# A bias load with a signal of its own, awaited ahead of the first scatter

## The chip, the cores and the metric

The kernel runs on one core of a Trainium2 chip. The metric is the device time of one execution in microseconds (us). The median of three runs of the kernel before is 1269.99 us (1265.9 to 1274.62).

## The reference, cut to what matters

One inference step of a hybrid layer: token mixers (gated delta rule and gated linear attention), a mixture of experts, and a final norm, all in float32, for 256 prompt tokens and 32 sample tokens. The mixture takes most of the time:

```
logits = x2d @ w_router + b_router                  # 288 tokens, 32 experts
top_v, top_i = lax.top_k(logits, 4); gates = softmax(top_v)
# for every expert e, over its tokens xe:
gu   = xe @ w_up[e] + b_up[e]                       # 1024 -> 2048
gate = minimum(gu[:, :1024], 7.0); up = clip(gu[:, 1024:], -7.0, 7.0)
act  = (up + 1.0) * gate * sigmoid(1.702 * gate)
yb   = act @ w_down[e] + b_down[e]                  # 1024 -> 1024
out[token] += yb * gates                            # then x += out, final rmsnorm by rms_final_w
```

## The kernel before

The five engines run programs of their own, ordered by semaphores written out by hand. After the token mixers and the router, the 32 experts are taken in 16 rounds of two experts, each expert with up to 64 token rows. The routine `two_experts` of each engine does one round.

**Weights.** A round needs 12 units of 2048 KB: four of w_up for each of the two experts, then two of w_down for each. They stream into a ring of eight slots. SP issues every load (`load_unit`, L354) in the order of use and, from unit 8 of the first round on (`refill`), each after a wait for the use that frees its slot. A unit of w_up is released by the last matmul that reads it. The units 0 to 7 of the first round are loaded while the mixers end; units 0 to 5 wait for places that the mixers free, unit 6 for slots of the state update, unit 7 (L375) for `out_done`, since its slot holds the new gated-delta state until POOL's store of it (L512, 2048 KB) has landed.

**SP's order around the change.** Four loads of the up bias into `b_gu` (L371), unit 6 (L373), the wait for `out_done`, unit 7, the wait for `yb_ok` (POOL's zeroing of `yr`, L514), the down bias into the first 32 rows of `yr` (L377, 128 KB), the final norm's gain into `wfin` on all partitions (L378, 512 KB), then the refills of units 8 to 11.

**TensorE.** After gathering the rows of the first two experts (`gather`, L999) it waits for `ld_bias` at 80, which counts the four loads of the up bias and the one of the down bias, 16 each (L1008), and for the last state update (L1009). Then the rounds: `up` of the first expert (bias matmuls at L958, weights at L971), in the first round only a turn of the gates, `scatter` (L950), `up` of the second expert, turns and gathers for the next round, `down` of both (L990). A scatter multiplies the matrix `S` by `yr`, the 128 output rows of the round before, and VectorE adds the result to `x2` (L1487). The first scatter takes no round's rows: `S` holds the gates and `yr` the down bias, zeros below, so that this product adds the down biases of all experts at once. Later scatters follow `rows_out`, which overwrites `yr`.

**wfin** is read at the end of the program only, behind a wait of VectorE for `ld_ffn` at 32; the first 16 of it are an early load of `wff`.

POOL issues its own stores of states: the gated-delta state (L512), then two of the prompt's and four of the sample's linear-attention state (L517, L521), 1152 KB in small rows.

Of the kernel before, what the change touches and what calls it, by code (L numbers as in the profile page):

```python
# [5 lines left out]
P = 128  # L6
# [21 lines left out]
E_N, TOPK, FF = 32, 4, 1024  # L28
# [8 lines left out]
def program(nc, a, o):  # L37
    ctx = ExitStack()
    with ctx:
# [3 lines left out]
        def sem(name):  # L43
            return ctx.enter_context(nc.semaphore(name))
# [21 lines left out]
        def share(s, rows, *shape):  # L66
# [50 lines left out]
        yr = xb[:, D:2 * D]  # L117
# [11 lines left out]
        wfin = hTf[:, 1280:1280 + D]  # L129
# [79 lines left out]
            rs8_ok qkn_ok p_qkT qkT_ok p_MA MA_ok p_y y_ok p_inv inv_ok  # L209
            p_tm p_ch ch_ok vd_ok p_smp g_abs g_exp g_lvl p_glvl p_low ag_ok  # L210
            ebl_ok zg_ok smk_ok smr_ok p_gkd kdg_ok p_gch gch_ok p_gs gsT_ok p_o0 p_gag og_ok slp_ok qs_e qs_ok sq_ok qksq_ok
            osq_ok o_ok p_oT oT_ok w_out w_out2 x_again p_x2 x2_ok xw_ok p_xnT
            xnT_ok p_lgT lgT_ok p_lg route_ok ss2_ok rs2_in xn_ok p_pos kdm_ok dec_ok p_up_s
            st_ok p_rows rows_ok hist_out out_done ld_ffn lg_ok tri_ok rnd_ok G_ok
            p_gat p_up p_yd p_sc p_S w_used gu_ok act_ok
# [17 lines left out]
        def place(n, odd):  # L233

            return (n + 4 * odd) % RING
# [21 lines left out]
        sems = {n: sem(n) for n in names}  # L257
# [38 lines left out]
        def _(sp):  # L296
# [50 lines left out]
            def load_unit(p, n, odd):  # L347

                if n < 8:
                    src = up[p * 2 + n // 4, n % 4 // 2, :, UNIT * (n % 2):UNIT * (n % 2 + 1)]  # L350
                else:
                    src = dn[p * 2 + (n - 8) // 2, n % 2]
                s = place(n, odd)
                sp.dma_start(slot[WSLOT[s]], src).then_inc(sems[f"ld_w{s}"], 16)  # L354
# [16 lines left out]
                sp.dma_start(b_gu[E_N * j:E_N * (j + 1)], a["b_up"][0, :, 512 * j:512 * (j + 1)]).then_inc(sems["ld_bias"], 16)  # L371
            sp.wait_ge(sems["p_up_s"], 4)
            load_unit(0, 6, 0)  # L373
            sp.wait_ge(sems["out_done"], 16 * 2)
            load_unit(0, 7, 0)  # L375
            sp.wait_ge(sems["yb_ok"], 1)
            sp.dma_start(yr[0:E_N], a["b_down"][0]).then_inc(sems["ld_bias"], 16)  # L377
            sp.dma_start(wfin, a["rms_final_w"].partition_broadcast(P)).then_inc(sems["ld_ffn"], 16)  # L378

            def refill(p, i, before, odd, n):  # L380

# [148 lines left out]
        def _(pe):  # L530
            c = Count(pe)

            def turn(out, src, n):

                return pe.transpose(out, src, ident[0:n, 0:n])  # L535
# [408 lines left out]
            def scatter(w, banks=(6, 7, 6, 7, 6, 7)):  # L944

                for at in range(6):
                    t, j = at // 2, at % 2
                    if banks[at] in banks[:at] or at < 2:
                        pe.wait_ge(sems["sc_ok"], w * 6 + max(at, 1))
                    pe.matmul(bank[banks[at]][0:TN[t], :], S[:, TO[t]:TO[t] + TN[t]], yr[:, 512 * j:512 * (j + 1)],  # L950
                              start=True, stop=True).then_inc(sems["p_sc"], 1)

            def up(i, q, k, odd):

                pe.wait_ge(sems["sel_ok"], i * 2 + (q + 1))
                for g in range(2):
                    rows_ = slice(64 * g, 64 * g + 64)
                    pe.matmul(bank[2 * q + g][:], sels[q][rows_].rearrange("p h c -> p (h c)"), b_gu[rows_], start=True, stop=False,  # L958
                              skip_group_check=True)
                for u in range(4):  # L960
                    n = 4 * q + u
                    if q == 0 and u % 2 == 0:
                        pe.wait_ge(sems["xe_ok"], i * 2 + (u // 2 + 1))
                    s = place(n, odd)
                    pe.wait_ge(sems[f"ld_w{s}"], landed(k, n, odd))
                    w = slot[WSLOT[s]].rearrange("p (k g h n) -> p k g h n", k=2, g=2, h=2)
                    for kk in range(2):
                        at = 2 * u + kk
                        for g in range(2):
                            for h in range(2):  # L970
                                last = pe.matmul(bank[2 * q + g][CAP * h:CAP * (h + 1), :], xeT[:, at, q * CAP:(q + 1) * CAP], w[:, kk, g, h, :],  # L971
                                                 start=False, stop=at == KT - 1, skip_group_check=True)
                    last.then_inc(sems["w_used" if u < 3 else "p_up"], 1)

            def act_t(q, w):

                pe.wait_ge(sems["act_ok"], w)
                for j in range(4):
                    last = turn(bank[5 - q][:, j * P:(j + 1) * P], by_cols(gu[:, 1])[:, :, j], P)
                last.then_inc(sems["p_at"], 1)  # L980

            def down(q, u, k, odd):

                n = 8 + 2 * q + u
                s = place(n, odd)
                pe.wait_ge(sems[f"ld_w{s}"], landed(k, n, odd))
                w = slot[WSLOT[s]].rearrange("p (k h n) -> p k h n", k=4, h=2)
                for kk in range(4):
                    for h in range(2):
                        last = pe.matmul(bank[5 - q][CAP * h:CAP * (h + 1), :], aTs[q][:, kk, CAP * u:CAP * (u + 1)], w[:, kk, h, :],  # L990
                                         start=u == 0 and kk == 0, stop=u == 1 and kk == 3, skip_group_check=True)
                last.then_inc(sems["w_used" if u < 1 else "p_yd"], 1)

            def gather(j, b):

                for n in range(4):
                    for t in range(NTT):
                        at = (4 * j + n) * P
                        last = pe.matmul(bank[b][:, n * P:(n + 1) * P], ot[:, t, at:at + P], G[:, t, :], start=t == 0, stop=t == NTT - 1)  # L999
                last.then_inc(sems["p_gat"], 1)  # L1000
# [4 lines left out]
            gather(0, 5)  # L1005
            pe.wait_ge(sems["lg_ok"], 5)
            gather(1, 4)
            pe.wait_ge(sems["ld_bias"], 80)  # L1008
            pe.wait_ge(sems["st_ok"], 6)  # L1009

            def two_experts(i, k, odd, first=False, last=False):

                up(i, 0, k, odd)
                if first:
                    pe.wait_ge(sems["gat_ok"], 1)
                    for t in range(NTT):
                        ins = turn(bank[5][0:E_N, TO[t]:TO[t] + TN[t]], gates[0:TN[t], E_N * t:E_N * (t + 1)], TN[t])
                    ins.then_inc(sems["p_gT"], 1)
                    pe.wait_ge(sems["rnd_ok"], 1)
                pe.wait_ge(sems["yb_ok"], i * 4 + 1)  # L1020
                pe.wait_ge(sems["S_ok"], i + 2)
                scatter(i)
                up(i, 1, k, odd)

                pe.wait_ge(sems["G_ok"], i * 2 + 2)
                for t in range(NTT):
                    ins = turn(bank[4][:, TO[t]:TO[t] + TN[t]], GG[0:TN[t], t, :], TN[t])
                ins.then_inc(sems["p_S"], 1)
                act_t(0, i * 2 + 1)
                if not last:  # L1030
                    pe.wait_ge(sems["G_ok"], i * 2 + 3)
                    pe.wait_ge(sems["sc_ok"], i * 6 + 7)
                    gather(0, 7)
                pe.wait_ge(sems["aT_ok"], i * 2 + 1)
                down(0, 0, k, odd)
                if last:
                    pe.wait_ge(sems["S_ok"], i + 3)
                    act_t(1, i * 2 + 2)
                    down(0, 1, k, odd)
                else:  # L1040
                    down(0, 1, k, odd)
                    pe.wait_ge(sems["S_ok"], i + 3)
                    act_t(1, i * 2 + 2)
                    gather(1, 6)
                pe.wait_ge(sems["aT_ok"], i * 2 + 2)
                down(1, 0, k, odd)
                down(1, 1, k, odd)

            two_experts(0, 0, 0, first=True)
            last = pe.value_load(rnd[0:1, 0:1], min_val=PAIRS // 2 - 1, max_val=5 * PAIRS // 2 - 1)  # L1050
            with pe.Fori(0, last) as m:
                two_experts(m * 2 + 1, m, 1)
                two_experts(m * 2 + 2, m + 1, 0)
# [789 lines left out]
```

## Time and profile before

| | before |
|---|---|
| median of the runs | 1269.99 us (3 runs, 1265.9 to 1274.62) |
| the profiled execution | 1268.15 us, its span 1266.4 us |
| TensorE (PE) busy | 1215.1 us, 96% |
| VectorE, ScalarE, GpSimd busy | 379.2, 215.3, 72.5 us |
| read from HBM, written | 428.39 MB, 4.88 MB |
| loads of w_up, w_down | 128 and 64 of 2048 KB |
| granted TensorE clock, mean | 0.979 |

Busy matmuls are pipelined and their ends are modelled, so a busy share of 96% doesn't say that TensorE is at its peak: matmuls behind a wait for weights also count as busy. The chain that ended last is followed back from the last instruction; at each step it names what released it. DMA share is the mean busy share of the core's 16 DMA engines; packets can overlap a little, so that a full stretch reads 1.0 or slightly above.

### The profile page before, as it was taken

Reading aid. Unit: us, or ns where it says so; the run is one execution under the profiler, and the core shown is the slowest. Engines: PE = TensorE matmul, PEld = TensorE weight load, DVE = VectorE, ACT = ScalarE, POOL = GpSimd, SP = SyncE. Lnnn points to the kernel's source line nnn. Section 1 sums busy time; section 2 is a strip of 40 time slices with the busy share of each in tenths; the row PEclk is TensorE's granted clock in tenths of the full one; section 3 lists DMA queues with packets and bytes.
Section 4 is the critical chain, followed back from the end, with each engine's and each line's share of the span. In section 5 each row is a group of like instructions: output and inputs, shape, how many; then the busy total and the mean of one; then the engine's idle time right before and its main releaser. Section 6 shows DMA issues by size and latency. Waiting matters only on the chain.

```text
span 1266.4 us, 15585 instructions
## 1 busy us (share of the span) xinstructions
PE 1215.1 (96%) x6209; PEld 591.7 (47%) x6209; DVE 379.2 (30%) x802; ACT 215.3 (17%) x522; POOL 72.5 (6%) x115
## 2 busy tenths in 40 slices
PE   6989999999599999999999999999999999999996
PEld 5777887757233434343433434343433424243432
DVE  3675874634030321212130321212130311212123
ACT  2144333412011101010111101010111101010102
POOL 5010103432000000000000000000000000000000
PEclk9999999897799999999999999999999999999999
DMA  9423010447699999999999999999999999999994
GB/s 270 138 84 120 7 68 1 146 171 308 230 399 427 427 427 427 429 428 429 428 427 430 429 427 427 430 429 428 428 430 429 427 429 430 429 427 429 429 429 195
DMA packets 49805, 433.75 MB, mean 343 GB/s; under 512 B 7422, under 2 KB 13898, under 8 KB 25196
## 3 DMA queue, kind: packets, MB, share of 16 engines
q1 hardware_dynamic: 48636, 429.59, 82.0%
q0 software_dynamic: 1136, 3.71, 1.0%
q8 instruction: 23, 0.38, 0.1%
q14 instruction: 10, 0.08, 0.0%
HBM read 428.39 MB, written 4.88 MB: 342 GB/s over the span
## 4 chain that ended last, share of the span: by engine, by line
PE 74%; DMA 19%; DVE 4%; ACT 1%; issue 1%; POOL 0%; DVEq 0%; SPq 0%; POOLq 0%; ACTq 0%
PE bank L971 30%; DMA ring<-in_w_up 13%; PE bank L990 11%; PE bank L950 7%; PE bank L999 4%; PE bank L594 4%; PE bank L535 3%; DMA ring<-in_w_down 3%; PE bank L686 3%; PE bank L864 2%; PE bank L958 2%; DMA out<-ring 1%; PE bank L743 1%; PE bank L765 1%; DMA xb<-in_b_down 1%
## 5 line engine op out<-in xcount | busy, mean ns | idle before, releaser
L971 PE MATMUL bank<-ring,xb 128*64 128x512 f32 x2048 | 450.6, 596 | 6.3 <-DMA ring<-in_w_up 6.3
L971 PEld LDWEIGHTS bank<-ring,xb 128*64 128x64 f32 x2048 | 144.6, 137 | 309.2 <-issue 299.6
L990 PE MATMUL bank<-ring,qkv 128*64 128x512 f32 x1024 | 227.2, 595 | 2.1 <-DMA ring<-in_w_down 1.4
L1487 DVE TENSOR_TENSOR qkv<-qkv,bank 128x512 f32<-128x512 f32 (+1 forms) x102 | 69.7, 683 | 295.0 <-PE bank L950 294.9
L990 PEld LDWEIGHTS bank<-ring,qkv 128*64 128x64 f32 x1024 | 70.7, 137 | 134.3 <-issue 127.7
L950 PE MATMUL bank<-xb,bT 128*128 128x512 f32 (+1 forms) x204 | 97.1, 611 | 1.6 <-DVE xb L1479 0.9
L999 PE MATMUL bank<-rowsel,ob 128*128 128x128 f32 x768 | 92.4, 278 | 0.0
L999 PEld LDWEIGHTS bank<-rowsel,ob 128*128 128x128 f32 x768 | 90.0, 195 | 0.3 <-issue 0.3
L1479 DVE COPY xb<-bank 64x512 f32<-64x512 f32 x16 | 11.1, 694 | 262.4 <-PE bank L990 262.4
L594 PE MATMUL bank<-hT,ring 128*128 128x288 f32 x320 | 81.0, 414 | 0.0
L1466 DVE TENSOR_SCALAR xb<-bank 128x512 f32<-128x512 f32 x32 | 21.8, 682 | 188.3 <-PE bank L535 188.3
L1769 ACT ACTIVATE qkv<-xb 128x512 f32<-128x512 f32 x32 | 20.2, 630 | 336.2 <-DVE xb L1466 334.1
L594 PEld LDWEIGHTS bank<-hT,ring 128*128 128x128 f32 x320 | 61.3, 193 | 17.6 <-issue 0.8
L1779 ACT COPY xb<-bank 64x512 f32<-64x512 f32 x48 | 27.8, 580 | 187.4 <-PE bank L990 187.0
L950 PEld LDWEIGHTS bank<-xb,bT 128*128 128x128 f32 (+1 forms) x204 | 26.8, 161 | 69.7 <-DVE qkv L1487 44.5
L524 POOL TENSOR_TENSOR rst<-rst,mhalf 128x1 f32<-128x1 f32 x3 | 2.6, 881 | 941.9 <-DVE rst L1562 941.8
L958 PE MATMUL bank<-hT 64*128 64x512 f32 x128 | 37.1, 656 | 13.6 <-DMA xb<-in_b_down 13.6
L1763 ACT ACTIVATE xb<-bank,wff 128x128 f32<-128x128 f32 x128 | 36.6, 369 | 55.1 <-PE bank L999 55.1
L1791 ACT COPY bT<-bank 128x288 f32<-128x288 f32 x16 | 6.4, 399 | 217.9 <-PE bank L535 217.9
L686 PE MATMUL bank<-hT,ring 128*128 128x288 f32 x128 | 40.0, 426 | 0.1
L864 PE MATMUL bank<-ring 128*128 128x512 f32 x64 | 30.8, 637 | 0.0
L535 PE MATMUL bank<-ident,xb 128*128 128x128 f32 x152 | 28.4, 305 | 1.6 <-DVE xb L1080 1.6
(342 smaller groups left out, 874.4 us busy)
## 6 DMA issues: line engine op xcount, KB each, us to landing
ring<-in_w_up SPq DMA_DIRECT2D x128, 2048.0 KB, 24.3
ring<-in_w_down SPq DMA_DIRECT2D x64, 2048.0 KB, 27.2
ring<-in_w_in SPq DMA_DIRECT2D x7, 2048.0 KB, 8.3
ring<-in_w_out SPq DMA_DIRECT2D x2, 2048.0 KB, 8.4
ring<-in_state_gdn SPq DMA_DIRECT2D x4, 512.0 KB, 10.0
out<-ring POOLq DMA_DIRECT2D x1, 2048.0 KB, 14.2
xb<-in_x_prompt SPq DMA_DIRECT2D x1, 1024.0 KB, 5.6
sls<-in_state_gla SPq DMA_DIRECT2D x4, 256.0 KB, 7.5
```

What stands on the lines that cost most here:

```text
L535: return pe.transpose(out, src, ident[0:n, 0:n])
L594: i = pe.matmul(bank[at % 4][:, 0:T], w[:, k, n * P:(n + 1) * P], hT[:, k, :], start=k == 0, stop=k == KT - 1)
L686: i = pe.matmul(bank[0][:, 0:T], w[:, k, n * P:(n + 1) * P], hT[:, k, :], start=k == 0, stop=k == KT - 1)
L864: i = pe.matmul(bank[b][:], z, w[:, k, :], start=k == 0, stop=k == KT - 1)
L950: pe.matmul(bank[banks[at]][0:TN[t], :], S[:, TO[t]:TO[t] + TN[t]], yr[:, 512 * j:512 * (j + 1)], start=True, stop=True).then_inc(sems["p_ ...
L958: pe.matmul(bank[2 * q + g][:], sels[q][rows_].rearrange("p h c -> p (h c)"), b_gu[rows_], start=True, stop=False, skip_group_check=True)
L971: last = pe.matmul(bank[2 * q + g][CAP * h:CAP * (h + 1), :], xeT[:, at, q * CAP:(q + 1) * CAP], w[:, kk, g, h, :], start=False, stop=at = ...
L990: last = pe.matmul(bank[5 - q][CAP * h:CAP * (h + 1), :], aTs[q][:, kk, CAP * u:CAP * (u + 1)], w[:, kk, h, :], start=u == 0 and kk == 0, ...
L999: last = pe.matmul(bank[b][:, n * P:(n + 1) * P], ot[:, t, at:at + P], G[:, t, :], start=t == 0, stop=t == NTT - 1)
L1487: v.tensor_tensor(d, d, bank[banks[at]][0:TN[t], :], ALU.add).then_inc(sems["sc_ok"], 1)
L1763: last = act.activation(xeT[:, k, :], bank[b][:, P * n:P * (n + 1)], ACT.Copy, scale=wff[:, k:k + 1])
L1779: act.copy(yr[CAP * q:CAP * (q + 1), 512 * h:512 * (h + 1)], bank[5 - q][CAP * h:CAP * (h + 1), :]).then_inc(sems["yb_ok"], 1)
```

## The change

The down bias gets a signal of its own, `ld_down`, in place of a name that nothing used. On SP, the load of wfin moves ahead of the wait for `out_done` and of unit 7, so that it follows unit 6; the down bias keeps its place behind unit 7 and the wait for `yb_ok`, and is now the last load ahead of the refills. TensorE waits ahead of the loop for the up bias alone (64), and, in the first round, for the down bias ahead of the first scatter, behind the first `up` and the turn of the gates.

```diff
-            osq_ok o_ok p_oT oT_ok w_out w_out2 x_again p_x2 x2_ok xw_ok p_xnT
+            osq_ok o_ok p_oT oT_ok w_out w_out2 x_again p_x2 x2_ok ld_down p_xnT
...
             sp.wait_ge(sems["p_up_s"], 4)
             load_unit(0, 6, 0)
+            sp.dma_start(wfin, a["rms_final_w"].partition_broadcast(P)).then_inc(sems["ld_ffn"], 16)
             sp.wait_ge(sems["out_done"], 16 * 2)
             load_unit(0, 7, 0)
             sp.wait_ge(sems["yb_ok"], 1)
-            sp.dma_start(yr[0:E_N], a["b_down"][0]).then_inc(sems["ld_bias"], 16)
-            sp.dma_start(wfin, a["rms_final_w"].partition_broadcast(P)).then_inc(sems["ld_ffn"], 16)
+            sp.dma_start(yr[0:E_N], a["b_down"][0]).then_inc(sems["ld_down"], 16)
...
             gather(1, 4)
-            pe.wait_ge(sems["ld_bias"], 80)
+            pe.wait_ge(sems["ld_bias"], 64)
             pe.wait_ge(sems["st_ok"], 6)
...
                     ins.then_inc(sems["p_gT"], 1)
                     pe.wait_ge(sems["rnd_ok"], 1)
+                    pe.wait_ge(sems["ld_down"], 16)
                 pe.wait_ge(sems["yb_ok"], i * 4 + 1)
                 pe.wait_ge(sems["S_ok"], i + 2)
                 scatter(i)
```

## Rows read from the trace of the kernel before

**Rows 1.** Page, part 2: what the DMA engines moved, in 40 equal slices of the span.
```profile
GB/s 270 138 84 120 7 68 1 146 171 308 230 399 427 427 427 427 429 428 429 428 427 430 429 427 427 430 429 428 428 430 429 427 429 430 429 427 429 429 429 195
```

**Rows 2.** Chain that ended last, late stretch. Columns: start us, length us, what.
```profile
1033.62 3.65 PE bank L971 x16
...
1058.15 34.15 DMA ring<-in_w_up
...
1092.34 3.65 PE bank L971 x16
...
1213.50 35.38 DMA ring<-in_w_down
...
1248.93 3.68 PE bank L990 x16
```

**Rows 3.** The same chain, ahead of the expert loop and in its first rounds.
```profile
307.15 14.24 DMA out<-ring
...
321.81 11.35 DMA xb<-in_b_down
...
333.20 2.08 PE bank L958 x4
335.28 16.02 PE bank L971 x64
...
352.43 5.76 PE bank L950 x12
...
359.25 13.88 PE bank L971 x64
...
394.44 1.06 PE bank L958 x4
...
451.27 1.06 PE bank L958 x4
```

**Rows 4.** Timeline of 296 to 375 us: start us, us, engine line op tiles [idle before].
```profile
302.79 18.97 SPq L354 DMA_DIRECT2D ring<-in_w_up  x2
...
312.51 7.10 PE L999 MATMUL bank<-rowsel,ob 128*128 128x128 f32 x48
...
319.65 1.14 ACT L1763 ACTIVATE xb<-bank,wff 128x128 f32<-128x128 f32 x4 [1.53 <-PE bank L999]
321.81 1.51 SPq L377 DMA_DIRECT2D xb<-in_b_down  x1
323.36 1.19 SPq L378 DMA_DIRECT2D hT<-in_rms_final_w  x1
...
341.04 10.63 SPq L354 DMA_DIRECT2D ring<-in_w_down  x4
...
363.11 10.97 SPq L354 DMA_DIRECT2D ring<-in_w_up  x4
```

**Rows 5.** Timeline of SP's queue alone, the first six weight units.
```profile
245.68 51.01 SPq L354 DMA_DIRECT2D ring<-in_w_up  x6
```

**Rows 6.** Windows: stretch, length, engines' busy us (count), PEclk, DMA share, GB/s.
```profile
300.00:320.00 20.00, 19.62 (x151) 18.18 (x150) 12.62 (x52) 7.55 (x13) 7.47 (x11) 0.66 1.01 384
320.00:326.00 6.00, 0.00 (x0) 0.00 (x0) 0.00 (x0) 0.80 (x4) 0.00 (x0) 0.71 0.98 265
326.00:332.00 6.00, 0.00 (x0) 0.00 (x0) 0.00 (x0) 0.00 (x0) 0.00 (x0) 0.50 0.94 331
332.00:342.00 10.00, 8.80 (x26) 2.59 (x28) 0.00 (x0) 0.00 (x0) 0.00 (x0) 0.62 0.07 27
342.00:344.00 2.00, 2.00 (x12) 0.70 (x10) 0.00 (x0) 0.00 (x0) 0.00 (x0) 1.00 0.95 238
...
362.00:366.00 4.00, 4.00 (x20) 1.29 (x18) 0.68 (x3) 0.00 (x0) 0.00 (x0) 1.00 0.57 164
...
400.00:1200.00 800.00, 795.11 (x3786) 312.90 (x3784) 165.34 (x364) 96.04 (x224) 0.00 (x0) 1.00 1.01 428
```

**Rows 7.** Tile in_w_up: time from issue to landing over its 128 loads.
```profile
DMA to landing us min/median/max: 7.2/24.3/34.4
```

## The prediction

> **What bounds the kernel now.** I read the page's slices first. From the thirteenth slice on (380 us) the DMA engines move 427 to 430 GB/s in every slice up to the last [rows 1]: one stream of expert weights. The reader is to see that this rate does not vary, whatever the engines do meanwhile.
>
> The chain that ended last says who waits for whom at the end. TensorE starts the same part of a round at 1033.62 and at 1092.34, so a round of two experts takes 58.72 us there, and the round holds one link in which a weight load is the cause, 34.15 us long; the last weight unit releases TensorE at 1248.93 [rows 2]. The end is set by the weight stream. Earlier it is not: between 394.44 and 451.27 a round takes 56.83 us and no load appears in the chain [rows 3]. TensorE alone needs 56.83 us a round, the stream 12 units of 2.097 MB (2048 KB), at the 428 GB/s of the slices [rows 1] 4.90 us each, 58.8 us. TensorE lives on the eight slots of the ring until its lead is used up, and from then on the stream decides. So whatever is gained ahead of the loop counts at the end only as far as the weight stream ends sooner.
>
> The same chain shows the place of the change. The state store occupies 307.15 to 321.39, then the down bias 321.81 to 333.16, then the first matmul of the loop at 333.20 [rows 3]. The timeline shows that TensorE had ended its gather at 319.61 (312.51 plus 7.10) and stood still for 13.59 us [rows 4]. SP's queue had issued units 0 to 5 by 296.69 [rows 5], and unit 6 at 302.79; unit 7 went out at 321.42, behind the store, b_down right behind it at 321.81, and wfin at 323.36 [rows 4]. The next weight unit (unit 8) goes out only at 341.04, when the first up unit has been used [rows 4].
>
> The windows show what that does to the stream. From 300 to 332 the DMA engines are full (shares 1.01, 0.98, 0.94), although at 265 to 384 GB/s, since the state stores are among the work; then 10 us with a share of 0.07, and again 4 us from 362 with 0.57; from 400 to 1200 the share is 1.01 [rows 6]. The first hole is the late first up. The second comes from the four units issued at 341.04 to 351.67 being drained before the next four are released at 363.11 [rows 4].
>
> **The change, part by part.**
>
> The wait ahead of the loop falls from 80 to 64: b_up alone. Its four loads stand ahead of unit 6 in SP's queue, issued before 302.79 [rows 4]; the 16.8 us to 319.61 exceed the shortest landing of a whole weight unit, 7.2 us, and the median under full load, 24.3, belongs to a queue of many units that is not there [rows 7]. Units 0 to 3 are older still. The other condition inside the first up is ScalarE's second half of the gathered rows, done at 320.79 [rows 4] and wanted half-way through, about 327. So TensorE starts at 319.65 and not at 333.20.
>
> It also runs faster. After the standstill the granted clock is 0.50 and only 0.62 over 332 to 342 [rows 6], the lower level of 1.2 GHz in part; the bias matmuls took 2.08 us against 1.06 later and the 64 up instructions 16.02 against 13.88 [rows 3]. Together 13.55 + 1.02 + 2.14 = 16.7 us for TensorE. The Trainium skill (TensorE: Matmul & The Clock Gate, section "Part 1: The HAM clock gate") states that a TensorE that stands still falls to half clock and gets it back by sustained work; the trace agrees (0.50 over 326 to 332), and by it 3.2 of those 16.7 us go with the wait. If the clock stayed low instead, the same work would cost those 3.2 us as before, and the sum below would still hold, as its slack shows.
>
> What the 16.7 us are worth is read from the stream. The first up ends each unit 3.47 us (13.88/4) after the one before: releases at 324.2, 327.6, 331.1, 334.6. The DMA engines are full until 332.7 (332 plus 0.07 x 10 us), so units 8 to 11 queue behind that work and run to 332.7 + 4 x 4.90 = 352.3. The fifth release needs the gate turn and copy (352.43 - 351.30 = 1.13 us), the scatter (5.76), the bias (1.06) and a unit (3.47) [rows 3]: 346.0, and its packets flow 1.1 us later (issue at 341.04; the share of 0.95 over 342 to 344 begins about 342.1): 347.1, with 5.2 us to spare. After that TensorE frees twelve slots in 56.83 us and the stream fills twelve in 58.8, so the lead grows. Both holes close.
>
> The size of the holes, from two sides. By engine time: 10 x (1.01 - 0.07) + 2 x (1.01 - 0.95) + 4 x (1.01 - 0.57) = 9.4 + 0.1 + 1.8 = 11.3 us [rows 6]. By bytes: 0.27 + 0.48 + 0.66 = 1.41 MB moved in those 16 us, at 428 GB/s 3.3 us' worth, so 12.7 us. I take 11.3, since engine time is what the stores and loads ahead of the hole use up and keep using.
>
> The wfin load moves ahead of the wait for the store, unit 7 and b_down. SP issues it (1.19 us) while it would wait until 321.4 anyway: nothing. Its 512 KB, at the 384 GB/s of 300 to 320 [rows 6], are 1.4 us of DMA that now stand before 332.7 rather than at its end; the full stretch ends at the same time. The store, unit 7 and b_down land up to 1.4 us later. If the engines were not full there, it would fill a gap, a gain of at most 1.4.
>
> b_down and the new wait. It goes out behind unit 7 as before and lands at 333.2 to 334.6 (11.35 us after issue, plus wfin's 1.4). TensorE comes to the new wait at about 335.1, ScalarE's copy follows the signal given ahead of it and ends at 335.7, so the wait costs 0. Queued behind it on TensorE are the scatter, the second up and all later releases; VectorE's gains wait for those. If b_down is late, the first 5.2 us of that are covered as above, and each further one opens a hole again. From below: no wait, and none of it gained. From above: b_down as slow as the median unit in the deep queue, 24.3 us [rows 7], plus 1.4: 347.5, 11.8 us late, 6.6 beyond the slack, gain 4.7. I take 0, as the row of b_down itself is nearest.
>
> The Trainium skill (DMA: Bandwidth & Descriptors, section "Queues, rings and completion order") states that each engine takes a queue's descriptors in ring order and turns between queues packet by packet; by it units 8 to 11, behind b_down in SP's queue, cannot hold it back, and only POOL's stores share with it. The trace agrees so far that 128 KB behind a 2 MB unit took 11.35 us.
>
> Sum: -11.3 us. The profiled execution took 1268.15 us, its span 1266.4 (1.75 around it), so 1256.9; the median of the runs shown, 1269.99, lies 1.8 above the profiled one, so 1258.7 on its scale.
>
> **Rivals.**
>
> A, the stream gains more. For it: TensorE is 16.7 us ahead, and 320 to 332 runs at 265 and 331 GB/s, mean 298 [rows 6]; if weight units queued behind unit 7 lifted that to 428, 12 x 130/428 = 3.6 us more: 15.0, hence 1255.0; with the full 16.7, 1253.3. Against: the engines' share there is already 0.94 to 0.98.
>
> B, b_down late. The wait moves from ahead of the loop to ahead of the scatter; two fifths of the stream's gain stay: 4.7, hence 1265.3. For it: it still stands behind unit 7, with wfin ahead too. Against: its own landing and 5.2 us of slack.
>
> C, the other side: b_down as late as the slowest unit, 34.4 us [rows 7]. 321.81 + 34.4 + 1.4 = 357.6, 21.9 behind 335.7, 16.7 beyond the slack; the hole is then larger than the 11.3 it replaced, slower by 5.4: 1275.4. It decides from a landing past 352.2. Nothing in the rows has such a queue ahead of 332.
>
> D, the change doesn't do it: another signal holds the first up. The latest seen is ScalarE at 320.79; even a hold until 327.6, 8 us, would open a hole of only 2.8 us beyond the slack. For no change it must last to 333. 1270.
>
> **How the numbers follow.** Forecast 0.72, its own range 1257.3 (12.7) to 1260.0 (10.0); A 0.13; B 0.10; C 0.02; D 0.03. The likeliest gives 1258.7. The three runs of before spread over 1265.9 to 1274.62, so I add some 2 us below A's mean and stop at B: 1253 to 1265.5. About 1% is what a measurement of this kernel can tell from no change; that is 12.7 us. All of A and a third of the forecast pass it: 0.13 + 0.24 = 0.37, as faster; C and a rest 0.03 as slower; the other 0.60 within.
>
> **What would show it.** Right: the first bias matmul at about 319.7; unit 8 issued at about 324, near unit 7; DMA share about 1.0 through 332 to 366; the first up at 13.9 us; b_down's landing at 333 to 335 and at most 1 us of TensorE idle ahead of the first scatter; the last unit's release at 1237.6 (1248.93 - 11.3). Links of weight loads enter the chain in an earlier round than before. Wrong: a link of b_down in the chain, a hole in the windows between 332 and 366, or a stream below 428 GB/s after it.

## The result and the profile after

The changed kernel takes 1258.9 us (median of nine runs, 1253.9 to 1268.67) against 1269.99 before: 0.9923 of before, with a 95% interval of 0.9895 to 0.9950, that is 9.8 us less (6.3 to 13.3). This ratio, which the text goes by, is not that of the two medians, which lie 11.1 us apart. Beside later experiments it ran again at 0.9921 (0.9890 to 0.9953) and at 0.9910 (0.9875 to 0.9946). The forecast was 1258.7, the gain forecast 11.3 us. All three ratios lie within 1% of before, their intervals on both sides of it. Of all runs below one is left out, a slow one of 2884.84 us among the eleven with the stores moved.

The profiled execution after took 1258.68 us, its span 1257.0, so 9.47 below the one of before. The slices of the page after, to be held against [rows 1]:

```profile
GB/s 271 137 82 119 14 68 1 95 224 251 367 427 427 426 429 427 428 430 428 429 428 428 430 427 430 429 428 428 430 428 429 428 429 430 427 429 429 427 427 185
```

A slice is 31.4 us here. The level is the same, but it is reached one slice earlier: the eleventh slice (314 to 346 us) moves 367 GB/s where it moved 230, the twelfth 427 where it moved 399.

The windows of after, in the same stretches as [rows 6] (length, engines' busy us, granted clock, DMA share, GB/s):

```profile
300.00:320.00 20.00, 19.22 (x129) 17.76 (x129) 11.57 (x41) 6.09 (x8) 5.66 (x8) 0.55 0.98 389
320.00:326.00 6.00, 6.00 (x41) 5.46 (x40) 1.81 (x13) 1.75 (x7) 2.25 (x4) 0.79 1.02 311
326.00:332.00 6.00, 6.00 (x30) 1.95 (x30) 0.00 (x0) 0.53 (x3) 0.00 (x0) 1.00 0.96 316
332.00:342.00 10.00, 9.32 (x45) 3.12 (x42) 0.00 (x0) 0.84 (x2) 0.00 (x0) 1.00 1.02 390
342.00:344.00 2.00, 2.00 (x6) 0.61 (x4) 1.26 (x2) 0.83 (x1) 0.00 (x0) 1.00 0.98 418
344.00:362.00 18.00, 18.00 (x76) 5.46 (x74) 6.45 (x16) 0.63 (x1) 0.00 (x0) 1.00 1.01 428
362.00:366.00 4.00, 4.00 (x35) 3.60 (x33) 2.46 (x4) 1.62 (x3) 0.00 (x0) 1.00 0.99 420
...
400.00:1200.00 800.00, 792.91 (x3775) 311.93 (x3774) 164.84 (x364) 96.05 (x224) 0.00 (x0) 1.00 1.01 428
```

The reader is to see the second column from the right. The stretch of 332 to 342 had a share of 0.07 and has 1.02; that of 362 to 366 had 0.57 and has 0.99; the stream of 400 to 1200 is as it was, 428 GB/s. Both holes are gone and no other appears.

SP's queue in the timeline of after (start us, length us, line, tiles):

```profile
303.79 1.73 SPq L371 DMA_DIRECT2D hT<-in_b_up  x4
307.50 0.35 SPq L354 DMA_DIRECT2D ring<-in_w_up  x1
307.89 0.43 SPq L374 DMA_DIRECT2D hT<-in_rms_final_w  x1
324.74 0.33 SPq L354 DMA_DIRECT2D ring<-in_w_up  x1
325.12 1.48 SPq L378 DMA_DIRECT2D xb<-in_b_down  x1
330.04 10.63 SPq L354 DMA_DIRECT2D ring<-in_w_down  x4
352.11 21.46 SPq L354 DMA_DIRECT2D ring<-in_w_up  x6
```

POOL's store of the state in the same timeline:

```profile
309.85 1.75 POOL L512 DMA_DIRECT2D out<-ring  x1 [6.37 <-DVE ring L1379]
```

Unit 8 follows unit 7 by 5.3 us (324.74 to 330.04), where it followed by 19.6 (321.42 to 341.04, [rows 4]). All that SP issues is some 3 to 5 us later than before, unit 6 at 307.50 against 302.79 and POOL's store of the state at 309.85 against 307.15: in this execution the mixers ended later, and the granted clock over 300 to 320 was 0.55 against 0.66. No instruction that the change touches lies ahead of that. From the start of the store to the last unit's release it is 1239.49 - 309.85 = 929.64 us against 1248.93 - 307.15 = 941.78 [rows 2, 3]: 12.1 less, of which the later store takes 2.7 back. Before and after, one execution each; the same stretch of the other executions stands at the end of the experiments.

The chain of after around the place, and at the end (start us, length us, what):

```profile
317.29 8.06 PE bank L999 x48
325.35 1.06 PE bank L958 x4
326.41 13.88 PE bank L971 x64
...
340.79 0.40 ACT bT L1786
341.19 0.25 issue
341.43 5.76 PE bank L950 x12
...
1239.49 3.68 PE bank L990 x16
```

TensorE goes from the gather straight into the bias matmuls, which take 1.06 us, not 2.08, and the first up takes 13.88, not 16.02 [rows 3]. ScalarE's copy, not the bias, releases the first scatter; no link of b_down is left in this chain. The tile's view says that the bias landed 12.5 us after its issue, at 337.6, and TensorE wanted it at 341.4:

```profile
DMA to landing us min/median/max: 12.5/12.5/12.5
```

### The profile page after: what moved, and what is told of

Its sections match the earlier page's. It is cut to its first block, busy times and chain, and to the rows that moved or that the text cites. A ratio compares the mean times of both kernels' runs of the same rounds, so it can differ in the third digit from the quotient of the medians.

```text
span 1257.0 us, 15585 instructions
## 1 busy us (share of the span) xinstructions
PE 1218.6 (97%) x6209; PEld 596.6 (47%) x6209; DVE 379.2 (30%) x802; ACT 215.2 (17%) x522; POOL 72.5 (6%) x115
## 4 chain that ended last, share of the span: by engine, by line
PE 74%; DMA 20%; DVE 4%; ACT 1%; issue 1%; POOL 0%; DVEq 0%; SPq 0%; POOLq 0%; ACTq 0%
PE bank L971 29%; DMA ring<-in_w_up 16%; PE bank L990 10%; PE bank L950 7%; PE bank L999 4%; PE bank L594 4%; PE bank L535 3%; DMA ring<-in_w_down 3%; PE bank L686 3%; PE bank L864 2%; PE bank L958 2%; PE bank L765 1%; PE bank L848 1%; PE bank L743 1%; PE bank L752 1%; PE bank L750 1%
## 5 line engine op out<-in xcount | busy, mean ns | idle before, releaser
L1480 DVE COPY xb<-bank 64x512 f32<-64x512 f32 x16 | 11.1, 694 | 262.4 <-PE bank L990 262.4
```

## The experiments

Two theories. **Stream**: the end is set by the weight stream; the change is worth the holes that it closes in it, and TensorE's earlier start is worth nothing beyond that. **Start**: the time follows how early and how fast TensorE enters the loop. A smaller rival gives wfin's move a part of the gain. Ratios are to runs of the kernel before on the same chip, medians 1271.67, 1271.48 and 1275.64 in the three groups. Each diff is against the changed kernel, that of wfin alone against the kernel before.

### The wait split alone

```diff
             load_unit(0, 6, 0)
-            sp.dma_start(wfin, ...)
             sp.wait_ge(sems["out_done"], 16 * 2)
...
             sp.dma_start(yr[0:E_N], a["b_down"][0]).then_inc(sems["ld_down"], 16)
+            sp.dma_start(wfin, ...)
```

> The wait is split as in the change, but wfin keeps its place behind b_down. Stream theory (the end is set by the weight stream, and the change closed the holes in it): wfin's 512 KB are the same DMA work on either side of unit 7, so the whole gain stays, about 11 us off the kernel before (1259 of 1270). Rival, wfin's move is part of the gain: 1.4 us or more of it is missing. In the profile: DMA share about 1.0 from 332 to 366, no wait for b_down ahead of the first scatter.

Measured: 1260.45 us, 0.9920 (0.9890 to 0.9949). The share of 332 to 342 is 1.02:

```profile
332.00:342.00 10.00, 9.32 (x45) 3.12 (x42) 0.00 (x0) 0.94 (x2) 0.00 (x0) 1.00 1.02 393
```

The gain comes from the split wait. A part of 1.4 us for wfin's place is smaller than the interval and is not excluded by these times; the next run bears on it, and so does the table at the end of the experiments.

### The wfin move alone

```diff
             load_unit(0, 6, 0)
+            sp.dma_start(wfin, ...)
...
             sp.dma_start(yr[0:E_N], a["b_down"][0]).then_inc(sems["ld_bias"], 16)
-            sp.dma_start(wfin, ...)
```

> Only wfin moves; TensorE still waits for the down bias ahead of the loop. Stream theory: the hole of about 11 us stays and b_down lands up to 1.4 us later, so 1270 to 1271.4, no change that can be told. Rival, wfin's move carries the gain: 1260 to 1265.

Measured: 1273.35 us, 1.0022 (0.9999 to 1.0044), so no gain. Its windows still have the hole, and TensorE stands still before it at the low clock:

```profile
326.00:334.00 8.00, 0.00 (x0) 0.00 (x0) 0.00 (x0) 0.00 (x0) 0.00 (x0) 0.50 0.83 311
334.00:344.00 10.00, 8.36 (x24) 2.44 (x26) 0.00 (x0) 0.00 (x0) 0.00 (x0) 0.60 0.01 3
```

### TensorE early, the stream late

```diff
+            sp.wait_ge(sems["w_used"], 4)
             for n in range(RING, 12):
                 refill(0, 0, 0, 0, n)
```

> The change, with SP holding back units 8 to 11 until the first unit of the second up is used. TensorE starts the loop as early as with the change, but the stream gets a hole of about 14.4 us (332.7 to 347.1 on the clock of the trace before), against 11.3 before. Stream theory: the gain is gone, 1270 to 1273. Rival, TensorE's earlier start (16.7 us) is what pays: 1253 to 1259, as with the change.

Measured: 1275.07 us, 1.0031 (1.0003 to 1.0058). This run separates the theories. The chain shows the loop entered as early and as fast as with the change (lines stand one further down), and the windows of the same execution show the stream's hole:

```profile
320.76 1.06 PE bank L959 x4
321.81 13.88 PE bank L972 x64
...
336.83 5.76 PE bank L951 x12
```

```profile
326.00:332.00 6.00, 6.00 (x30) 2.01 (x28) 0.00 (x0) 0.00 (x0) 0.00 (x0) 1.00 0.91 348
332.00:348.00 16.00, 15.32 (x59) 4.69 (x57) 7.71 (x17) 2.30 (x3) 0.00 (x0) 1.00 0.03 11
348.00:352.00 4.00, 4.00 (x22) 1.37 (x20) 0.00 (x0) 0.00 (x0) 0.00 (x0) 1.00 0.94 315
```

TensorE is busy over the whole stretch (15.32 of 16 us, granted clock 1.00), the DMA engines are not (0.03), and the time is that of the kernel before and a little more, 4.0 us (0.4 to 7.4). That fits the larger hole: by bytes, as in the prediction, the 0.18 MB of 332 to 348 leave 15.6 us empty, against 12.7 before. The start pays nothing that these runs can tell.

### The down bias behind one unit, and behind four

```diff
-            sp.dma_start(yr[0:E_N], a["b_down"][0]).then_inc(sems["ld_down"], 16)
-            for n in range(RING, 12):
+            refill(0, 0, 0, 0, RING)
+            sp.dma_start(yr[0:E_N], a["b_down"][0]).then_inc(sems["ld_down"], 16)
+            for n in range(RING + 1, 12):
                 refill(0, 0, 0, 0, n)
```

> The change, with the down bias loaded behind unit 8. It lands 4 to 6 us after TensorE reaches the new wait. Stream theory: that lies within or just beyond the slack of 5.2 us, so the time of the change stays to within 1 us (1259 to 1260), while TensorE shows the wait ahead of the first scatter. Rival, every us of TensorE's start counts: 4 to 6 us above the change, 1263 to 1265.

Measured: 1259.18 us, 0.9906 (0.9870 to 0.9942), beside the change at 0.9921. The wait is there and costs nothing that can be told. The chain of its profiled execution (1267.83 us, the longest of its six):

```profile
332.48 3.61 PE bank L972 x16
...
336.52 14.24 DMA xb<-in_b_down
350.76 0.09 issue
350.85 7.20 PE bank L951 x12
358.05 1.06 PE bank L959 x4
```

The first up would have let the scatter begin at about 347.5 (332.48 + 13.88, and the 1.13 of the turn and copy), so TensorE stood for 3.3 us. The scatter then took 7.20 us, not 5.76 (the granted clock was 0.86 over 350 to 362), so that the second up began 4.8 us late, within the slack of 5.2. The windows show a trace of a hole at the place where the fifth release is due, 0.4 us (2 x 0.21):

```profile
350.00:362.00 12.00, 11.15 (x30) 3.62 (x32) 7.16 (x15) 0.63 (x1) 0.00 (x0) 0.86 1.00 425
362.00:364.00 2.00, 2.00 (x12) 0.72 (x10) 0.55 (x3) 0.00 (x0) 0.00 (x0) 1.00 0.80 320
```

With all four units ahead of the bias:

```diff
-            sp.dma_start(yr[0:E_N], a["b_down"][0]).then_inc(sems["ld_down"], 16)
             for n in range(RING, 12):
                 refill(0, 0, 0, 0, n)
+            sp.dma_start(yr[0:E_N], a["b_down"][0]).then_inc(sems["ld_down"], 16)
```

> The change, with the down bias loaded behind units 8 to 11. It lands about 19 us after TensorE reaches the new wait, 13.7 us beyond the slack of 5.2, and TensorE restarts at half clock, up to 3 us more. Stream theory: a hole of 14 to 17 us comes back, 1272 to 1276. Rival, TensorE's start pays in full: 19 to 22 us above the change, 1278 to 1281.

Measured: 1272.64 us, 1.0009 (0.9981 to 1.0037). The bias is awaited from about 341.4 (the first up's end at 340.27 and the 1.13) until 358.67, 17.3 us; the stream then runs empty:

```profile
326.36 13.91 PE bank L971 x64
...
340.65 18.02 DMA xb<-in_b_down
```

```profile
340.00:356.00 16.00, 0.70 (x5) 0.20 (x3) 0.00 (x0) 1.67 (x2) 0.00 (x0) 0.67 1.00 426
356.00:372.00 16.00, 13.24 (x39) 4.20 (x40) 7.71 (x17) 0.63 (x1) 0.00 (x0) 0.80 0.04 14
```

While TensorE stands, the stream is full (1.00); 16 us later, when TensorE works, it is empty (0.04), a hole of 15.5 us. The gain is gone, as in the forecast's rival C, though the time is about 1 us above before and not the 2 to 6 expected; the interval reaches to 4.7 us. By the prediction's own sum a stand of 17.3 us costs 17.3 - 5.2 - 11.3 = 0.8 us against before. So a bias that came 3.3 us late was free, and one that came 17.3 us late took the gain away; between the two nothing was run.

### The stores out of the way

This asks whether taking DMA work out of the full stretch ahead of the stream moves the end. POOL's stores of slp and sls become SP's, behind the last weight unit:

```diff
-            g.wait_ge(sems["gch_ok"], 2)          # POOL, ahead of the loop
-            ... 2 stores of slp; wait for st_ok; 4 stores of sls
...
             for n in range(12):
                 refill(PAIRS - 1, last * 2 + 1, last * 2, 1, n)
+            sp.wait_ge(sems["gch_ok"], 2)
+            ... the same 6 stores
```

> The changed kernel once more, beside the next three on one chip. About 0.992 of before, near 1259 of 1270.

Measured: 1260.29 us, 0.9921 (0.9890 to 0.9953). In this execution the mixers ended some 6 us earlier than in the one shown above (the first bias matmul at 319.18 against 325.35), and the down bias was the last to come, by little: the scatter began at 335.40, where the copy alone would have let it begin at about 335.25 (319.18 + 1.06 + 13.88 + 1.13).

```profile
322.93 12.39 DMA xb<-in_b_down
335.31 0.09 issue
335.40 5.76 PE bank L950 x12
```

> The change, with POOL's stores of the linear-attention states (slp and sls, 1152 KB) issued by SP behind the last weight unit instead of ahead of the loop, where those stores moved 281 GB/s alone (321 to 324 us of the trace before): 4.2 us of DMA work leave the full stretch ahead of the stream, and TensorE's work is the same. Stream theory: 4 us below the change, near 1255, as the last 17 us of the kernel have room for the stores. Rival, TensorE's start sets the time: no difference to the change, 1259.

Measured: 1260.05 us, 0.9911 (0.9878 to 0.9945). That is 1.3 us below the change beside it by the ratios and 0.2 by the medians; the intervals are too wide to tell either from 0 or from the 4 expected. The profiled executions tell more. The one here can be laid over that of after: its chain has the bias matmuls' work begin 0.15 us later (the first up at 326.56 against 326.41). Its last unit is released at 1238.16, 1.33 earlier, in this one pair. Its windows show where the rest went:

```profile
320.00:332.00 12.00, 12.00 (x68) 7.53 (x69) 1.93 (x14) 2.29 (x8) 0.00 (x0) 0.89 0.83 305
...
332.00:350.00 18.00, 17.29 (x67) 5.35 (x65) 5.91 (x9) 2.30 (x3) 0.00 (x0) 1.00 0.98 418
350.00:356.00 6.00, 6.00 (x30) 2.01 (x28) 1.80 (x9) 0.00 (x0) 0.00 (x0) 1.00 0.71 265
```

The stretch does not end sooner; it gets holes. Unit 7 still waits for the store of the big state, out at 324.72 against 324.74, and the small stores had filled the time around it: 12 x 0.17 = 2.0 us empty. And units 8 to 11, drained sooner, end before the fifth release: 6 x 0.30 = 1.8 us. Together 3.8 of the 4.2 us that were taken out by the estimate. My expectation treated the stretch ahead of the stream as one heap of work; two waits stand in it.

Then wfin as well:

```diff
             load_unit(0, 6, 0)
-            sp.dma_start(wfin, ...)
...
             for n in range(12):
                 refill(PAIRS - 1, last * 2 + 1, last * 2, 1, n)
+            sp.dma_start(wfin, ...)
+            ... the 6 stores
```

> As the run before it, and wfin too is loaded behind the last weight unit: another 1.4 us of DMA work out of the way of the stream. Stream theory: 5.6 us below the change, near 1253.4. Rival, TensorE's start sets the time: 1259. If wfin or the stores are late at the end, VectorE waits for wfin or the last store ends the span, and the time is above the run before it.

Measured: 1256.42 us, 0.9892 (0.9853 to 0.9932); the interval overlaps that of the change beside it, so it was run again in a third group, with the change and with wfin alone behind the last unit (the same edit without the stores):

> The changed kernel, beside the next two on one chip: 0.992 of before.

> The change, with wfin alone loaded behind the last weight unit; the stores stay with POOL ahead of the loop. Stream theory: 1.4 us of DMA work leave the full stretch, so at most 1.4 us below the change, and less where the stretch then runs empty before the next slot is free, as it did when the stores alone were moved. Rival, no difference to the change.

> Stores and wfin behind the last unit, once more for a closer interval: 2 to 4 us below the change beside it, 0.989 to 0.990 of before; holes of some 2 to 3 us ahead of unit 7 take back part of the 5.6 us of DMA work removed. Rival, the earlier gap to the change was chance: 0.992.

Measured in that group: the change 1263.98 us, 0.9910 (0.9875 to 0.9946); wfin alone last 1259.57, 0.9880 (0.9857 to 0.9903); stores and wfin last 1255.57, 0.9843 (0.9817 to 0.9870). The last interval lies below that of the change beside it; over all runs the medians are 1260.62 us (27 runs) and 1256.28 (11). So stores and wfin behind the last unit beat both kernels, against the change by 3.7 us in one group and 8.5 in the other, the latter more than the 5.6 us of work that was taken out. For wfin alone the intervals overlap, and its 3.8 us (0.0030 x 1275.64) are more than its 1.4 us of work: how much of the gain is wfin's and how much the stores' stays open. The windows of the repeated run show the same two holes:

```profile
324.00:328.00 4.00, 4.00 (x31) 3.12 (x32) 0.00 (x0) 2.28 (x8) 0.00 (x0) 1.00 0.55 170
...
350.00:356.00 6.00, 6.00 (x30) 2.01 (x28) 2.98 (x10) 0.63 (x1) 0.00 (x0) 1.00 0.73 265
```

In the first run of this kernel only the first of them is there (a share of 0.56 over 324 to 330), and the stretch of 350 to 356 is full (1.02).

The times of one kernel spread over some 15 us, as the last section shows, and most of that comes from ahead of the place of the change. The stretch from the start of POOL's store of the state to the last unit's release leaves it out. It is read from the chain and the timeline of each profiled execution, one for each row:

| kernel | store starts, us | last unit released, us | between, us |
|---|---|---|---|
| before | 307.15 | 1248.93 | 941.78 |
| wfin alone moved | 309.02 | 1250.36 | 941.34 |
| the change | 309.85 | 1239.49 | 929.64 |
| the change, second group | 306.75 | 1237.19 | 930.44 |
| the change, third group | 311.55 | 1240.95 | 929.40 |
| wait split alone | 309.82 | 1239.13 | 929.31 |
| refills held back | 308.25 | 1252.63 | 944.38 |
| down bias behind one unit | 318.95 | 1248.65 | 929.70 |
| down bias behind four | 312.84 | 1256.74 | 943.90 |
| stores last | 310.01 | 1238.16 | 928.15 |
| wfin last | 319.46 | 1248.34 | 928.88 |
| stores and wfin last | 312.76 | 1237.36 | 924.60 |
| the same, third group | 311.34 | 1239.59 | 928.25 |

With the hole closed the stretch is 11.3 to 12.5 us shorter than before, whether wfin moves or not; wfin's move alone makes it 0.4 shorter. Stores, wfin or both at the end take 0.5 to 2.3 us more off it, in one execution 4.8 to 5.8. So the 8.5 us of the third group are not in the stream of the execution profiled there. Two executions of the last kernel differ by 3.7 us in this stretch; why was not tried.

## Why the prediction was right

**What bounds the kernel.** Right: held back with TensorE already in the loop, the stream takes the gain away. The level of 428 GB/s over 400 to 1200 is the same in all thirteen profiled executions.

**TensorE's 16.7 us.** Seen in full: no standstill, 1.06 and 13.88 us. The rule of the Trainium skill (TensorE: Matmul & The Clock Gate, section "Part 1: The HAM clock gate") says that a TensorE that stands still falls to half clock and that sustained work gives it back. The first half agrees with the runs: the granted clock is 0.50 over 326 to 334 with wfin alone moved, where TensorE stands still. The second half is not borne out ahead of the loop: over 300 to 320 of after TensorE was busy for 19.22 of 20 us and was granted 0.55. In the loop it has 1.00 from 326 on. As the sum had it, those us are not the gain.

**The holes, 11.3 to 12.7.** Both closed. From the store on, the stretch is 12.1 us shorter, between the two estimates, and in three more executions with the hole closed 11.3 to 12.5 us; the runs give 9.8 (6.3 to 13.3), which doesn't tell the two apart. That the single pair of executions differs by only 9.47 is the 2.7 us by which the later one had fallen behind before the store.

**wfin.** Right in that it brings nothing by itself: from the store to the last release the split wait gives 929.31 us without its move and 929.40 to 930.44 with it, the kernel before 941.78 without and 941.34 with. That it makes b_down up to 1.4 us later was not borne out, as the next point shows.

**b_down and the new wait.** Forecast: 11.35 + 1.4 = 12.75 us after issue and no wait to speak of. Measured: 12.5 and 12.4 us, a wait of none and of about 0.2. The number is right by luck, for the term added to 11.35 was another. The 1.4 us of wfin don't show: with wfin ahead of the bias but no weight unit soon behind it, it landed after 10.9 us with the refills held back, and after 10.96 with wfin alone moved:

```profile
324.64 10.96 DMA xb<-in_b_down
```

With units 8 to 11 behind it in the queue it took 12.4 to 12.8 us in five executions, wherever wfin stood, and 7.4 to 7.9 with POOL's small stores out of the way. So the units behind it held it back by 1.4 to 1.9 us, where the prediction had inferred that they cannot; by what means stays open. Ahead of it they held it back more (14.24 us behind one unit, 18.02 behind four), as the rule of the Trainium skill has it, by which each engine takes a queue's descriptors in ring order (DMA: Bandwidth & Descriptors, section "Queues, rings and completion order"). The slack was put at 5.2; a stand of 3.3 us, 4.8 with the slower scatter, was free to within 0.4, one of 17.3 was not.

**The signs.** Most came as named, some 2 to 6 us later on the trace's clock, since the mixers ended later. Weight loads first hold up the chain at 873.87 us, where they did at 941.82 before, and at 811.11 and 815.79 in two more executions: one round earlier and two. With the wait split alone they do so at 930.82, in the same round as before. One sign of being wrong, a link of b_down in the chain, did come, in the second group's execution; the wait behind it is 0.15 us, so that sign was drawn too sharply.

**The rivals.** A (15 us or more) lies outside the first two intervals, which end at gains of 13.3 and 14.0 us, though not outside the third (15.9); the held-back refills speak against its reason, TensorE's start, and the table's 11.3 to 12.5 us against its size. B is excluded by the windows. C was brought about on purpose by four units ahead of the bias: it removes the gain as forecast, at 15.5 us of hole; its 5.4 us above before belong to a stand of 21.9 us, which no run has.

**Where the reasoning was too simple.** The prediction treated 300 to 332 as full of work that can only shift. That held for the change, and the sum needed no more. It failed for my own experiment with the stores: there the stretch is held by a store's landing and by slot releases, and in the one pair of executions that can be laid over each other only 1.3 of some 4.2 us came through.

## What to carry to other kernels

When a kernel ends on a stream of loads, price a wait by the hole that it leaves in the stream, not by the time that the waiting engine stands: hold the stream back with the engine running, and the gain is gone. A wait can be moved to a place behind which the stream has work queued; how late it may then be is the length of that queue less the time to the next release. Taking other DMA work out of the way pays only as far as the stream can move up at once.

## What the runs showed of the hardware

The spread between runs of one kernel follows TensorE's mean granted clock. Over 68 runs of the kernel before, the shortest, 1265.27 us, had 0.981 and the longest, 1281.31, 0.967: some 1.1 us for each 0.001. In all thirteen profiled executions the clock is 1.00 from 380 us to 1240. The difference lies ahead of that: the execution with the down bias behind one unit took 1267.83 us, that of the change 1258.68, 9.15 more, and its store of the state starts 9.10 later (318.95 and 309.85). On the way there TensorE, busy for 37.41 of 40 us in both, was granted 0.70 over 200 to 240 in the one and 0.91 in the other. Why the clock falls earlier in one execution than in another was not tried. The spread is as large as the effect of this change, so a single pair of runs could have shown any sign.
